# Four blocks of a small float32 transformer on one core: root chain, mask and weight splits moved in VectorE's order, half-wise hand-over of x

## What is computed

```
x = x + gdn_mixer(norm(x));   x = x + swiglu(norm(x))      # first mixer: gated delta rule, 16 value heads
x = x + mla_mixer(norm(x));   x = x + swiglu(norm(x))      # second: latent attention, 8 heads
x = rms_norm(x, final_norm)
x = x + diff_attention(norm(x)); x = x + swiglu(norm(x))   # third: differential attention, 8 heads
x = x + swa_sink_attention(norm(x)); x = x + swiglu(norm(x))   # fourth: sliding window, 16 query, 4 key heads
```

## Time and profile before

| | |
|---|---|
| median of 3 runs | 1457.49 us (1457.11 to 1457.64) |
| profiled execution | 1455.18 us, span in the trace 1453.4 us |
| TensorE busy | 1413.3 us, 97% |
| VectorE busy | 924.4 us, 64% |
| ScalarE busy | 727.1 us, 50% |
| mean granted clock of TensorE | 0.989 |
| HBM read | 214.26 MB |

### The profile page before, as it was taken

One profiled execution on the slowest core, in us unless ns is written; L12 is line 12 of the kernel. 1 busy time (PEld: TensorE's weight loads), 2 busy tenths in 40 slices (PEclk: granted clock), 3 DMA queues, 4 the chain that ended last, 5 costly groups with the idle time before them and its releaser, 6 DMA issues.

```text
span 1453.4 us, 19865 instructions
## 1 busy us (share of the span) xinstructions
PE 1413.3 (97%) x7787; PEld 1204.3 (83%) x7787; DVE 924.4 (64%) x1630; ACT 727.1 (50%) x1245; POOL 21.4 (1%) x44
## 2 busy tenths in 40 slices
PE   8999999899999999999999999899999999999999
PEld 8998989788888888888888878678888877888887
DVE  6866767646755547656555499875554586665553
ACT  7554535334544435545444375745444565454442
POOL 4100000000000000000000000000000000000000
PEclk9999999999999999999999999999999997999999
DMA  9432322224566554526665545236655541366652
GB/s 243 118 106 81 87 82 86 69 70 154 178 184 184 187 179 154 172 72 205 188 188 184 179 159 175 73 116 203 188 188 188 162 147 56 115 191 187 188 188 87
DMA packets 168838, 216.61 MB, mean 149 GB/s; under 512 B 11219, under 2 KB 136746, under 8 KB 168746
## 3 DMA queue, kind: packets, MB, share of 16 engines
q1 hardware_dynamic: 166976, 213.03, 47.2%
q10 hardware_dynamic: 1770, 2.32, 0.5%
HBM read 214.26 MB, written 1.05 MB: 148 GB/s over the span
## 4 chain that ended last, share of the span: by engine, by line
PE 79%; DVE 16%; ACT 2%; issue 2%; DMA 1%; ACTq 0%; SPq 0%; DVEq 0%
PE psum L898 21%; PE psum L900 21%; PE psum L899 21%; DVE w_low L646 4%; PE psum L1112 4%; PE psum L1296 2%; PE psum L1104 2%; PE psum L1272 2%; PE psum L1233 1%; DVE work L2304 1%; PE psum L1118 1%; PE psum L1285 1%; DMA ring<-in_gdn_w_in 1%; DVE work L818 1%; PE psum L889 1%
## 5 line engine op out<-in xcount | busy, mean ns | idle before, releaser
L646 DVE TENSOR_TENSOR w_low<-ring,w_high 128x1024 fp32r<-128x1024 f32 (+3 forms) x395 | 474.2, 1211 | 323.7 <-ACT w_high L632 321.9
L632 ACT ACTIVATE w_high<-ring 128x1024 fp32r<-128x1024 f32 (+3 forms) x395 | 411.4, 1048 | 442.0 <-PE psum L900 430.2
L898 PE MATMUL psum<-w_high,hT 128*128 128x512 f32 (+2 forms) x944 | 372.8, 395 | 0.6 <-DVE hT L2099 0.6
L900 PE MATMUL psum<-w_high,hT 128*128 128x512 f32 (+2 forms) x944 | 366.8, 389 | 0.0
L899 PE MATMUL psum<-w_low,hT 128*128 128x512 f32 (+2 forms) x944 | 366.3, 388 | 0.0
L898 PE MATMUL psum<-w_high,parts 128*128 128x512 f32 (+1 forms) x532 | 208.2, 391 | 0.3 <-DVE work L2655 0.3
L900 PEld LDWEIGHTS psum<-w_high,hT 128*128 128x128 f32 x944 | 177.7, 188 | 36.8
L898 PEld LDWEIGHTS psum<-w_high,hT 128*128 128x128 f32 x944 | 178.1, 189 | 34.7 <-DVE hT L2099 0.9
L899 PEld LDWEIGHTS psum<-w_low,hT 128*128 128x128 f32 x944 | 178.1, 189 | 34.0
L900 PE MATMUL psum<-w_high,parts 128*128 128x512 f32 (+1 forms) x532 | 206.0, 387 | 0.0
L899 PE MATMUL psum<-w_low,parts 128*128 128x512 f32 (+1 forms) x532 | 205.7, 387 | 0.0
(11 more groups left out here) (278 smaller groups left out, 1413.2 us busy)
## 6 DMA issues: line engine op xcount, KB each, us to landing
ring<-in_ffn_w_gate_up SPq DMA_DIRECT2D x176, 256.0 KB, 3.2
ring<-in_w_gate_up SPq DMA_DIRECT2D x176, 256.0 KB, 3.2
ring<-in_gdn_w_in SPq DMA_DIRECT2D x48, 512.0 KB, 3.9
ring<-in_ffn_w_down SPq DMA_DIRECT2D x44, 512.0 KB, 3.3
ring<-in_w_down SPq DMA_DIRECT2D x44, 512.0 KB, 3.3
ring<-in_da_w_qkv SPq DMA_DIRECT2D x24, 512.0 KB, 4.0
ring<-in_gdn_w_out SPq DMA_DIRECT2D x16, 512.0 KB, 3.3
ring<-in_mla_w_out SPq DMA_DIRECT2D x8, 512.0 KB, 4.5
```

The lines of the kernel that those rows point to most:

```text
L632: nc.scalar.activation(piece_slot(w_high, n), piece_slot(ring, n), ACT.Copy).then_inc(s.w_hi, 1)
L646: nc.vector.tensor_tensor(piece_slot(w_low, n), piece_slot(ring, n), piece_slot(w_high, n).bitcast(F32), ALU.subtract).then_inc(s.w_lo, 1)
L898: mm(out, lhs[0], rhs[0], start=start, stop=False)
L900: return mm(out, lhs[1], rhs[0], start=False, stop=stop)
```

## The change

Nothing is computed otherwise. Three parts:

1. **x by halves.** `residual` counts `x_ready` after each 512-column half, and `turn_x` waits for each half by itself. ScalarE's `square_sums` and VectorE's `final_gains` wait for the second half as before.
2. **First mixer.** In the prelude TensorE makes tile 3 ahead of the gates; ScalarE and VectorE run taps and convolutions earlier and splits later. `other_scales(0)` and two splits go from ahead of group 0 to its level 1. `other_scales(g + 1)` goes ahead of the wait for the last outputs, `gate_causal(g + 1)` from level 5 to behind the levels, the split of tile `at + 4` from level 3 to level 4, and for group 3 the splits and query products of level 1 go to level 2.
3. **Fourth mixer.** The keys are turned in the second half of the queries, and the four splits ahead of the rounds go into rounds 3 to 6, one each, on ScalarE and on VectorE.

```
@@ turn_x
-                pe.wait_ge(s.x_ready, 2 * TURN[k] + t + 1)
                 for h in range(2):
+                    pe.wait_ge(s.x_ready, 4 * TURN[k] + 2 * t + h + 1)
@@ tensor: prelude of the first mixer
-            tile(1)
-            tile(2)
+            for i in range(1, 4):
+                tile(i)
...
             gate_rows(0)
-            tile(3)
             turned_masks()
@@ tensor: fourth mixer
-            def keys_turned(r):
-                if r == 3:
...
+            def queries_turned(t, r):
+                if (t, r) == (0, 1):
                     pe.wait_ge(s.sw_roped, 1)
                     fill_bank(pe, tp_sq, 0)
                     fill_bank(pe, tp_sq, 1)
@@ scalar: prelude
-            split_high(act, tile_piece[0] + SPLIT)
-            tiles(1)
-            tiles(2)
+            tap(1)
+            tap(2)
+            for i in range(3):
+                split_high(act, tile_piece[i] + SPLIT)
+            tap(3)
+            silu(0)
             act.wait_ge(s.gcum_ready, 1)
             gate_diff(0)
+            silu(1)
+            tap(4)
             gate_exp(0)
...
@@ scalar: fourth mixer
-            for n in range(12):
+            for n in range(8):
...
+            def beside_round(i):
+                if i == 2:
+                    empty_bank(act, tp_sq, 5, 1)
+                elif 3 <= i < 7:
+                    split_high(act, a_kv + 5 + i + SPLIT)
@@ vector: residual
                     last = tt(at, B[4 + 2 * t + h][:, :], at, ALU.add)
-                last.then_inc(done, 1)
+                    if done == s.x_ready:
+                        last.then_inc(done, 1)
@@ vector: prelude
             first_level(0)
             first_y(0)
-            split_low(dve, tile_piece[7] + SPLIT)
-            other_scales(0)
+            split_low(dve, tile_piece[4] + SPLIT)
+            split_low(dve, tile_piece[5] + SPLIT)
@@ vector: beside_level
-                if lv == 1:
+                if lv == (1 if more else 2):
...
                     query_products(g)
                     if g and more:
                         tiles(at)
-                elif lv == 2:
+                    elif not g:
+                        other_scales(0)
+                        split_low(dve, tile_piece[6] + SPLIT)
+                        split_low(dve, tile_piece[7] + SPLIT)
+                if lv == 2:
...
-                        tiles(at + 4)
+                        conv(at + 4)
                 elif lv == 4 and more:
+                    split_low(dve, tile_piece[at + 4] + SPLIT)
                     tiles(at + 5)
...
-                    if more:
-                        gate_causal(g + 1)
@@ vector: behind the levels
                 if more:
+                    gate_causal(g + 1)
                     key_scales(g + 1)
...
                 tt(pairs(gd_o[g][:, 0, :]), pairs(B[2][:, :]), rq[0], ALU.mult)
+                if more:
+                    other_scales(g + 1)
                 dve.wait_ge(s.o_psum, g * 2 + 2)
...
-                if more:
-                    other_scales(g + 1)
@@ vector: fourth mixer
-            for n in range(12):
+            for n in range(8):
...
+                elif i < 7:
+                    split_low(dve, a_kv + 5 + i + SPLIT)
```

More of the change, by code:

```diff
@@ L1524, in keys_turned @@
                     fill_bank(pe, tp_sq, 1)
-            def queries_turned(t, r):
-                if (t, r) == (1, 2):
+                elif (t, r) == (1, 2):
                     pe.wait_ge(s.q_roped, 1)
@@ L1533, in _ @@
             by_tokens(a_kv, HALF, lambda t: B[t], k=7)
-            by_tokens(a_swq, HALF, lambda t: B[2 + t], before=keys_turned)
+            by_tokens(a_swq, HALF, lambda t: B[2 + t])
             by_tokens(a_swq + 4, HALF, lambda t: B[t], lambda t: pe.wait_ge(s.sw_copied, t + 1), before=queries_turned, half=s.q_half)
@@ L1587, in square_sums @@
             def square_sums(k, t):
-                act.wait_ge(s.x_ready, 2 * TURN[k] + t + 1)
+                act.wait_ge(s.x_ready, 4 * TURN[k] + 2 * t + 2)
                 if t and k not in GAINED:
@@ L1803, in _ @@
             f(eg1, gcum[:, 1, :], ACT.Exp).then_inc(s.eg_ready, 1)
-            tiles(3)
-            silu(0)
-            tiles(4)
-            silu(1)
-            tiles(5)
+            split_high(act, tile_piece[3] + SPLIT)
+            tap(5)
             squares_kq(0)
+            tap(6)
+            split_high(act, tile_piece[4] + SPLIT)
+            split_high(act, tile_piece[5] + SPLIT)
             silu(2)
-            tiles(6)
-            tiles(7)
+            tap(7)
+            split_high(act, tile_piece[6] + SPLIT)
+            split_high(act, tile_piece[7] + SPLIT)
             silu(3)
@@ L2020, in query_squares @@
                 f(sw_squares[:, c, t, :], w_q[:, t, c * HALF:(c + 1) * HALF], ACT.Square).then_inc(s.sw_sq, 1)
-            for n in range(12):
-                if n == 7:
-                    empty_bank(act, tp_sq, 1, 1)
+            for n in range(8):
                 split_high(act, a_kv + n + SPLIT)
@@ L2037, in _ @@
                         queries_out(0, t)
+                    empty_bank(act, tp_sq, 1, 1)
                     act.wait_ge(s.sw_copied, 4)
@@ L2049, in _ @@
             query_squares(1, 1)
-            attention(sw_rounds, True, lambda i: empty_bank(act, tp_sq, 5, 1) if i == 2 else None)
+            def beside_round(i):
[3 more added lines that the diff above has]
+                    split_high(act, a_kv + 5 + i + SPLIT)
+            attention(sw_rounds, True, beside_round)
             empty_banks(act, tp_so, 1)
@@ L2080, in residual @@
                     last = tt(at, B[4 + 2 * t + h][:, :], at, ALU.add)
-                last.then_inc(done, 1)
+                    if done == s.x_ready:
+                        last.then_inc(done, 1)
+                if done != s.x_ready:
+                    last.then_inc(done, 1)
             def final_gains(t):
                 dve.wait_ge(s.late_loaded, 32)
-                dve.wait_ge(s.x_ready, 2 * TURN[5] + t + 1)
+                dve.wait_ge(s.x_ready, 4 * TURN[5] + 2 * t + 2)
                 tt(xy[:, t, :], x[:, t, :], gfin, ALU.mult).then_inc(s.y_ready, 1)
@@ L2436, in _ @@
             stt(gl, tmp32[0], -1.0, alog.unsqueeze(1).to_broadcast([P, T, VH]), ALU.mult, ALU.mult).then_inc(s.gl_ready, 1)
+            conv(1)
             split_low(dve, tile_piece[0] + SPLIT)
-            tiles(1)
             dve.wait_ge(s.gcum_psum, 1)
@@ L2442, in _ @@
             tt(ed0, B[4][:, T * VH:T * VH + VH], gcum[:, 0, :], ALU.subtract).then_inc(s.gcum_ready, 1)
-            tiles(2)
-            tiles(3)
+            conv(2)
+            split_low(dve, tile_piece[1] + SPLIT)
+            conv(3)
+            split_low(dve, tile_piece[2] + SPLIT)
             dve.wait_ge(s.mask_psum, 1)
             v.tensor_copy(const("level")[:, P:(1 + STEPS) * P], B[2][:, 0:STEPS * P]).then_inc(s.mask_ready, 1)
+            conv(4)
             gate_causal(0)
@@ L2449, in _ @@
             own(ts(neg_eg1, eg1, -1.0, None, ALU.mult))
-            tiles(4)
-            tiles(5)
+            split_low(dve, tile_piece[3] + SPLIT)
+            conv(5)
             key_scales(0)
-            tiles(6)
+            conv(6)
             key_products(0)
@@ L2719, in _ @@
             dve.wait_ge(s.tables_made, 2)
-            for n in range(12):
-                if n == 7:
-                    empty_bank(dve, tp_sq, 0, 0)
+            for n in range(8):
                 split_low(dve, a_kv + n + SPLIT)
@@ L2727, in _ @@
                 elif n == 7:
+                    empty_bank(dve, tp_sq, 0, 0)
                     dve.wait_ge(s.sw_copied, 4)
```

## The result

| | before | after |
|---|---|---|
| median | 1457.57 us (1457.11 to 1458.19, 4 runs) | 1442.14 us (1440.62 to 1442.56, 4 runs) |
| profiled execution, span | 1455.18, 1453.4 us | 1442.56, 1440.8 us |
| TensorE busy | 1413.3 us, 97% | 1410.2 us, 98% |
| mean granted clock | 0.989 | 0.992 |

The ratio is 0.990 (95% interval 0.9888 to 0.9912): 15.4 us, or 1.1%, faster. The forecast was 1442.0 us. The two profiled executions differ by 12.6 us only. The kernel before, in all 48 of its executions that stood beside this study's runs, on several chips, took 1453.24 to 1459.25 us with a median of 1455.84, so the four of the first comparison are on its high side. The changed kernel itself was timed beside those four only; against the median of the 48 it would be 13.7 us faster, so 13 to 15 us is as close as the size of the gain is known.

A forecast was written before the change was run, and what follows sets the result against it. TensorE is busy 97% of the span, so only its idle time (40 us) and lower-clock time can be won. The terms sum to 15.5 us, taken from the median 1457.49 to give 1442.0 us; range 1435 to 1453.

The forecast's parts named there:

- one of its own signs: Fourth mixer: the forecast is wrong if the clock's lower level sits in rounds other than 0 to 2.
- Prelude: Start of the first mixer: waits for gates and SiLU and lost clock go, a mask wait of 1.3 comes; +3.2 us.
- Group 0: First mixer: chain and two splits at level 1 make y late, costing a wait and lower clock; -3.0 us.
- 2.4 of wait: Level 1 of group 0: y comes 3.1 us late, less 0.7 slack, so TensorE waits 2.4 us.
- Groups 1 to 3: First mixer: TensorE's waits on VectorE go, with some clock won back; +2.9, +3.6 and +3.9 us.
- Halves: Turned x (L889): waiting per half saves up to 0.64 us each, part given back at hT; +2.2 us.
- Fourth mixer: First maps start 4.1 us earlier, rounds with splits give back 1.4; +2.7 us.
- a round is about 0.35 longer: Fourth mixer, rounds 3 to 6: a split each nearly fills ScalarE and VectorE, lengthening rounds past 3.60; -1.4 us.
- C: Groups 1 to 3: waits only move, half their gain is lost, about 5 us; 1447 us, chance 0.14.
- A: Fourth mixer's rounds stay at 2.4 GHz and group 0's wait costs no clock; 1437.8 us, chance 0.23.
- B: Fourth mixer: VectorE makes TensorE wait some 2.9 us in round 2, lower clock in rounds 3 to 7; 1452, chance 0.15.
- D: Group 0's new 2.4 us wait sets a lower clock that stays over levels and rounds; slower, 1466 us, chance 0.03.

The follow-up runs named there:

- run 9: The changed kernel with the prelude and group 0 as before on all engines; 1439.25 us against 1454.98 for the kernel before, ratio 0.9894.
- run 7: The changed kernel with GpSimd's table products held until level 1 of group 0 is done; 1439.88 us against 1455.61 for the kernel before.
- run 4: The kernel before with only other_scales(g + 1) moved ahead of the wait for the last outputs; 1451.9 us against 1455.28, ratio 0.9971.
- run 5: The kernel before with gate_causal(g + 1) behind the levels, a split moved to level 4, group 3's splits and query products in level 2; 1447.94 us against 1456.37.
- run 3: The kernel before with only the fourth mixer's part (keys turned later, four splits in rounds 3 to 6); 1452.31 us against 1455.28.
- run 11: The changed kernel with fourth-mixer splits moved: ScalarE's beside rounds 0 and 2, VectorE's in rounds 2 (two), 3 and 4; 1438.65 us against 1454.98 before.
- run 8: The changed kernel with group 0's root chain at level 2 and splits spread over levels 2 to 4; 1439.89 us against 1455.61 before.
- run 2: The kernel before with x handed over by halves and nothing else; 1454.56 us against 1455.28, ratio 0.9991.

## Why the prediction was right, and where its terms were not

The time was 1442.14 us for a forecast of 1442.0, inside the range, and the mechanism (TensorE's waits on work that VectorE did too early) is the one that was forecast. The exact hit is luck in two ways: the four executions of before lay high, and errors of both signs cancelled. By one of its own signs the forecast was wrong in part: the lower level does sit in a round other than 0 to 2, the one from 1222 us on.

*Prelude, forecast 3.2, found 3.1.* The sum is right and its parts are not. The new wait at the turned masks is 0.91, not 1.3, and L1367 and L1041 have no wait. But 1.7 of clock and 1.25 of SiLU are two gains only together: run 9 shows that with the old order of ScalarE what is won at the clock is waited for at the SiLU. What made the 3.1 is that ScalarE came to `silu(0)` sooner (its table load starts at 29.84 us, before at 37.38). The extra table load cost TensorE nothing that the profile shows: L1041 has no wait, and the ACTIVATE behind each of the two loads begins within 0.02 us of its end.

*Group 0, forecast -3.0, found -5.3.* This is the term that failed most. The step was "2.4 of wait" and "rounded up to 1.0" of clock. The wait was 4.60. The 2.4 holds when GpSimd is quiet (2.58 in run 7); I had priced the chain and the splits at their lengths in the earlier trace rows and not looked at what GpSimd does at the place to which they move. The clock cost 1.9 us against the kernel before, not 1.0, as the lower level lasted over L1086 and L1052. And one gain was not in the forecast: the 0.82 of wait for a convolution went. -4.60 - 1.9 + 0.41 + 0.82 = -5.3. Prelude and group 0 are one trade, of about -2 us in the profiles.

*Groups 1 to 3, forecast 10.4, found 11.7.* The root chain fits the idle time of 2.79, of which 0.40 is left, and run 4 alone gave 3.4 of the 3.9. Group 1's terms hold to 0.1. The excess is clock: I took 0.7 and 0.8 for the two stretches behind 256 and 290 us, and they cost 1.3 and 1.5 (run 5). The first one also lies behind the state product of group 2, at 255.73, so it counts in group 3: that is why group 2 won 3.0 and not 3.6. In group 3 the new wait is 1.31, forecast 1.1, at the product behind the masked p. Runs 4 and 5 alone gave 3.4 and 8.4 us, 11.8 together.

*Halves, forecast 2.2,* found 1.6 up to the fourth mixer's x, with the give-back at hT as described (0.60 to 1.03); 0.7 alone with an interval of 0 to 2.6 us.

*Fourth mixer, forecast 2.7, found 1.2 in the profiles and 3.0 in run 3.* The first maps start 4.4 us earlier (4.1 forecast): 1.27 for the keys, 1.5 at the first scores, and 1.6 because VectorE comes to the first maxima 1.8 us behind the first scores and not 3.4. Before, and now:

```profile
1200.83 1.01 DVE L2202 TENSOR_REDUCE small<-psum 128x2 f32<-128x256 f32 x2
...
1185.27 1.02 DVE L2213 TENSOR_REDUCE small<-psum 128x2 f32<-128x256 f32 x2 [0.76 <-PE psum L1277]
```

The wait of the maps is 1.43 as before all the same, because the scores ahead of it ran at the full clock and took TensorE 3.3 us instead of 4.9. What failed is the other half, "a round is about 0.35 longer", -1.4, with "the clock at 0.50 for the same rounds as before". From the first maps to the output weights it takes 39.4 us, and before 36.2: -3.2. A round with a split is 0.2 longer, but a split in round 5 delays `sw_write` by 1.5 in place of 0.65, VectorE's norm makes TensorE wait 1.5 in round 2, and the clock falls behind both. Run 11 takes 3.0 us back, though its wait in round 2 stays. That the loads of the ring move along with the splits cost nothing, as forecast: in the round at 1212.24 us 139 GB/s arrive, and no wait of TensorE from x to the output weights is for a split.

*The rivals.* C does not hold: the waits did not move, as groups 1 to 3 show. A and B each describe a part: the clock fell for fewer rounds at first, VectorE made TensorE wait in round 2, and the clock fell again behind it, for one round, not five. D's mechanism was there (a wait of group 0 that drops the clock), at 1.9 us instead of 9. Adding the parts run alone, 0.7 + 3.0 + 3.4 + 8.4 = 15.5 us, less the 2.2 of prelude and group 0, gives 13.3, between the 12.6 of the profiles and the 15.4 of the medians; each part is known to 1.5 or 2 us only, so this doesn't prove that they add up. Not tested alone: the prelude without group 0, which can't be separated since it defers the very splits that group 0 then does.

## What to carry to other kernels

Where one engine is busy 97%, list its waits by who ended them, and look in the helper's timeline for idle time just ahead of the late work: a chain of small instructions moved in front of a wait, where its engine stood idle anyway, gave 3.4 us for two lines. Work put off is not work saved: before counting a gain at its old place, read all engines, GpSimd too, at the new one. A split in round 5 stood ahead of a step that TensorE waited for, and run 11, with all splits in rounds 0 to 4, took 3.0 us less from the first scores on.

## What the hardware showed that was not expected

GpSimd's products on SBUF more than double VectorE's smallest instructions beside them in group 0 (0.17 to 0.38 us; 0.24 beside the second set of products in run 8), and lengthen a split from 1.18 to 1.40; the second set itself takes 3.67 us beside the splits and 1.71 in run 8. In the two profiles of the kernel before, the waits of the first mixer repeat within 0.1 us, and the spread of 1453.24 to 1459.25 us of this kernel goes with its mean granted clock (0.993 at the shortest, 0.987 to 0.989 at the four longest). The clock fell behind a wait of 1.95 us at 27 us and 2.08 in run 2, but not behind 1.86 and 1.66 at the same place in runs 9 and 5, nor behind 2.7 in run 8. A short stretch at the lower level cost 1.7 us at 28 us, 1.3 at 256 and 1.5 at 290 in the kernel before. Why one wait of 1.4 us is followed by the lower level (1188 us) and another not (1.42 at 1197 us in run 3) is left open.
